# Pooled half first: a mix that starts before the heads are scaled, in a two-layer decoder trunk

## What is computed

```python
h = rmsnorm(x, norm1)
proj = h @ w_in                                  # q, k, v, o: 4 x 512; u_pool: 512; 8 gates
hm = mlstm(q, k, v, gates, state)                # 4 heads of width 128
hm = hm * lax.rsqrt(jnp.mean(hm * hm, axis=-1, keepdims=True) + EPS)
hm = hm.reshape(B, T, MLSTM_WIDTH) * mlstm_norm * o
zp = pool_mixer(u_pool, ...)                     # windows 2/4/8/16, w_pool, pool_scale
mix = jnp.concatenate([hm, zp], axis=-1) @ w_out # 1024 -> 1024
x = x + mix
x = x + peer_ffn(rmsnorm(x, norm2), ...)         # 8 heads x 16 of 16384 experts for each token
x = x + sigmoid(x @ w_gate) * (p @ w_ple)
```

## Time and profile before

| | |
|---|---|
| median of 3 runs | 1942.24 us (1940.42 to 1944.46) |
| the profiled execution | 1939.56 us, its span 1937.8 us |
| busy share of the span | PE 53%, DVE 57%, ACT 9%, POOL 60% |
| TensorE clock granted, mean | 0.762 of full speed |
| chain that ended last | DMA 32%, POOL 24%, PE 17%, DVE 15%, issue 11% |
| moved | 687.24 MB, 553.72 MB of it by the gathers |

### The profile page before, as it was taken

The page is one execution under the profiler, slowest core; times in us unless marked ns, Lnnn a source line. Parts: engine busy times, 40 slices in busy tenths (PEclk is TensorE's granted clock), DMA queues, the critical chain, the costliest instruction groups (busy, mean ns, idle before and its releaser), DMA issues.

```text
span 1937.8 us, 18049 instructions
## 1 busy us (share of the span) xinstructions
PE 1034.4 (53%) x6274; PEld 477.3 (25%) x6274; DVE 1095.3 (57%) x2851; ACT 173.9 (9%) x297; POOL 1156.0 (60%) x1062
## 2 busy tenths in 40 slices
PE   7867230574754654717655766465854640035556
PEld 3433120332311232304111333332311120021113
DVE  1266898867920467888800486968950179960001
ACT  2222010000100011100000022101100010000001
POOL 0033556254677766676677767456576787777770
PEclk9888665687878876758778978777876675568888
DMA  7577767697999999999999999899799999999993
GB/s 294 190 297 283 260 223 283 181 380 294 385 409 409 409 413 412 372 377 353 410 409 409 405 407 408 275 359 399 256 401 410 409 404 409 409 409 409 409 409 144
DMA packets 173192, 687.24 MB, mean 355 GB/s; under 512 B 19856, under 2 KB 21520, under 8 KB 158366
## 3 DMA queue, kind: packets, MB, share of 16 engines
q0 software_dynamic: 152064, 553.72, 73.1%
q1 hardware_dynamic: 21038, 132.37, 18.0%
HBM read 679.88 MB, written 6.59 MB: 354 GB/s over the span
## 4 chain that ended last, share of the span: by engine, by line
DMA 32%; POOL 24%; PE 17%; DVE 15%; issue 11%; ACT 1%; SPq 0%; DVEq 0%; ACTq 0%; POOLq 0%
POOL rows L1182 24%; DMA rows<-in_v,index_tb 10%; DMA rows<-in_u,index_A 7%; PE bank L728 7%; DMA rows<-in_v,index_ta 7%; PE acc L1010 6%; DMA rows<-in_u,index_B 4%; DVE rows L1747 4%; DMA wring<-in_w 1%; DVE scratch L1570 1%; DMA rows<-in_v,index_S 1%; DVE scratch L1644 1%; PE bank L725 1%; DVE scratch L1694 1%; DVE scratch L1693 1%
## 5 line engine op out<-in xcount | busy, mean ns | idle before, releaser
L1182 POOL DMA_INDIRECT rows<-in_u,index_A x256 | 325.3, 1271 | 365.6 <-DVE index_A L1722 178.4
L1010 PE MATMUL acc<-rows,wz 128*32 128x512 f32 x2048 | 341.4, 798 | 289.2 <-DMA rows<-in_v,index_tb 142.8
L728 PE MATMUL bank<-wring,turned 128*128 128x512 f32 x832 | 410.3, 645 | 69.9 <-DVE decayed L1454 33.0
L1182 POOL DMA_INDIRECT rows<-in_u,index_B x256 | 299.8, 1171 | 108.8 <-issue 71.0
L1747 DVE SCALAR_TENSOR_TENSOR rows<-rows,xn_a 128x1024 f32<-128x1024 f32 x256 | 304.7, 1224 | 79.9 <-DMA rows<-in_u,index_A 76.6
L1182 POOL DMA_INDIRECT rows<-in_v,index_ta x256 | 252.6, 987 | 145.0 <-PE acc L1010 78.2
L1747 DVE SCALAR_TENSOR_TENSOR rows<-rows,xn_b 128x1024 f32<-128x1024 f32 x256 | 306.9, 1226 | 56.7 <-DMA rows<-in_u,index_B 51.1
L1182 POOL DMA_INDIRECT rows<-in_v,index_tb x256 | 242.3, 946 | 107.7 <-issue 61.9
L728 PEld LDWEIGHTS bank<-wring,turned 128*128 128x128 f32 x832 | 165.6, 208 | 272.5 <-issue 245.9
L1010 PEld LDWEIGHTS acc<-rows,wz 128*32 128x32 f32 x2048 | 74.0, 127 | 532.9 <-issue 510.7
L1780 DVE TENSOR_TENSOR x_b<-x_b,acc 128x1024 f32<-128x1024 f32 x2 | 2.4, 1222 | 260.6 <-PE acc L1010 260.6
(11 more groups left out here) (293 smaller groups left out, 997.5 us busy)
## 6 DMA issues: line engine op xcount, KB each, us to landing
wring<-in_w SPq DMA_DIRECT2D x108, 1024.0 KB, 8.1
scratch<-in_c_s SPq DMA_DIRECT2D x2, 2064.0 KB, 11.1
out_c_s<-scratch SPq DMA_DIRECT2D x2, 2064.0 KB, 9.9
rows<-in_u,index_A POOLq DMA_INDIRECT x256, 11.4
rows<-in_v,index_ta POOLq DMA_INDIRECT x256, 7.7
rows<-in_u,index_B POOLq DMA_INDIRECT x256, 9.2
rows<-in_v,index_tb POOLq DMA_INDIRECT x256, 7.9
keys<-in_keys SPq DMA_DIRECT2D x2, 1024.0 KB, 9.8
```

The source lines that it names most:

```text
L728: ins = pe.matmul(ps[:, :], turned["A"][:, 4 * h + c, :], w[:, c, :], start=first, stop=end, skip_group_check=True)
L1010: ins = pe.matmul(acc[i * QUAD:(i + 1) * QUAD, c, :], wz[:, i, g * QUAD:(g + 1) * QUAD], row, start=first, stop=end, skip_group_check=True)
L1182: pool.indirect_dma_start(out=rows[:, n % RING, :], out_offset=None, in_=a[table], in_offset=bass.IndirectOffsetOnAxis(ap=which[:, at:at + ...
```

## The change

In the mix, half h = 0 becomes the pooled inputs and half h = 1 the heads: `half_index` swaps the two halves of the weights for the mix, and `dense` reads the other half of `turned`. The mix's first block now waits for the pooling alone; the wait for the heads moves to `(j, h) == (0, 1)`. In the list of pass 0, the h = 0 halves of both blocks stand ahead of `scale_heads` and `heads`. In the other passes `scale_heads` of the large tile goes behind `weigh_keys`, pooling goes ahead of the sample tile's `scale_heads` and `heads`, and the halves (0, 0) of the mix go ahead of these too. The planner's tables are unchanged, `dense` takes one source, and its waits are otherwise as before.

```diff
@@ stage_front
     add("norm_heads", big)
-    add("scale_heads", big)
     if p:
         add("weigh_keys", big)
     else:
         add("pool_r", big)
         add("pool", big)
+        for j in range(2):
+            add("mix", p, j, 0, big)
+    add("scale_heads", big)
     add("heads", big)
...
         add("norm_heads", t)
-        add("scale_heads", t)
-        add("heads", t)
     for t in tiles if p else []:
         add("pool_r", t)
     for t in tiles if p else []:
         add("pool", t)
-    for j in range(2):
-        for h in range(2):
-            for t in tiles:
-                add("mix", p, j, h, t)
+    for t in tiles if p else []:
+        add("mix", p, 0, 0, t)
+    for t in small:
+        add("scale_heads", t)
+        add("heads", t)
+    for j, h in ((0, 1), (1, 0), (1, 1)) if p else ((0, 1), (1, 1)):
+        for t in tiles:
+            add("mix", p, j, h, t)
@@ half_index
-    return {"project": IN0, "mix": OUT0, "query": PQ0, "gate": GATE0}[e[0]] + 2 * e[2] + e[3]
+    h = 1 - e[3] if e[0] == "mix" else e[3]
+    return {"project": IN0, "mix": OUT0, "query": PQ0, "gate": GATE0}[e[0]] + 2 * e[2] + h
@@ dense
-                        for s in source:
-                            for i in range(1 if kind == "S" or not parts else parts):
-                                emptied(pe, *((s, t, i) if parts else (s, t)))
+                        for i in range(1 if kind == "S" else parts):
+                            emptied(pe, *((source, t, i) if parts > 1 else (source, t)))
...
+                chunk = 4 * (1 - h if name == "mix" else h)
...
-                        ins = pe.matmul(ps[:, :], turned["A"][:, 4 * h + c, :], w[:, c, :], start=first, stop=end,
+                        ins = pe.matmul(ps[:, :], turned["A"][:, chunk + c, :], w[:, c, :], start=first, stop=end,
@@ mix
-                dense("mix", p, j, h, t, ("heads", "pool_z"), 0)
+                if (j, h) == (0, 1):
+                    emptied(pe, "heads", t)
+                dense("mix", p, j, h, t, "pool_z", 1)
```

More of the change, by code:

```diff
@@ L724, in dense @@
                         for g in range(4):
-                            ins = pe.matmul(ps[lane_group(g), 0:P], turned["S"][:, 4 * h + c, :], w[:, c, g * P:(g + 1) * P],
+                            ins = pe.matmul(ps[lane_group(g), 0:P], turned["S"][:, chunk + c, :], w[:, c, g * P:(g + 1) * P],
                                             start=first, stop=end, skip_group_check=True)
                     else:
-                        ins = pe.matmul(ps[:, :], turned["A"][:, 4 * h + c, :], w[:, c, :], start=first, stop=end,
+                        ins = pe.matmul(ps[:, :], turned["A"][:, chunk + c, :], w[:, c, :], start=first, stop=end,
                                         skip_group_check=True)
@@ L767, in project @@
             def project(p, j, h, t):
-                dense("project", p, j, h, t, ("turn",), 2)
+                dense("project", p, j, h, t, "turn", 2)
             def cumulate(t):
@@ L909, in query @@
             def query(p, j, h, t):
-                dense("query", p, j, h, t, ("turn2",), 2)
+                dense("query", p, j, h, t, "turn2", 2)
             def turn_pq(t, j):
@@ L1018, in gate @@
             def gate(p, j, h, t):
-                dense("gate", p, j, h, t, ("turn3",), 2)
+                dense("gate", p, j, h, t, "turn3", 2)
             def embed(p):
```

## The result

The changed kernel takes 1949.86 us (median of 20 runs, 1944.21 to 1957.09) and the kernel before, in the runs beside it, 1940.53 us (20 runs, 1936.61 to 1948.46). The forecast was +9.0 us and 1951.2 us. The profiled execution of the changed kernel took 1945.72 us, its span is 1943.9 us, at a mean granted clock of 0.767.

The account below looks back on a forecast made before the run. It took the DMA engines, full at about 410 GB/s, as the bound, so only longer dry times of the gather queue cost. 0.6 + 2.3 + 6.5 - 0.7 + 0.3 = +9.0 on 1942.24 gave 1951.2 us, range 1944.5 to 1957.5.

Parts of the forecast that it names:

- Pass 2's v group, +6.5: Tile 1's first v group waits 16.7 us longer for wz, 10.2 us is refunded: +6.5 us, ends 0 and +16.7.
- The refund: Pass 2: four weight halves travel while the gathers stand still, instead of inside the v stream, giving back 10.2 us.
- Pass 2's earlier mix, -0.7: Pass 2: mix starts some 1.35 us earlier, second addition 0.6 us late, so 0.7 us kept; ends 0 and 3.
- Pass 0, +0.6: Pass 0's mix starts 0.86 us earlier, but head transposes in its middle add 1.50 us; ends +0.3 and +1.5.
- the upper end: Pass 0: transposes stay at the slow 1.06 us and the earlier start buys one more slow matmul pass, 0.43 us: +1.5.
- Pass 1, +2.3: Pass 1: dots ahead of the last choose delay the states' load, store and mix weights by 2.3 us; ends 0 and +3.
- Pass 3, +0.3: Pass 3: mix starts no sooner, one PE transpose costs +0.3 us, engines stay full; ends -12 and +5.1.
- a sign of a wrong forecast: Pass 3's last u row moving by over 3 us more than pass 2's end does.
- the third rival: Pass 3 loses its four rows too, +5.1 us: +14.1 in all, 1956.3 us; chance 0.14.
- the rule on the shared port: VectorE and GpSimd share an exclusive port pair, causing Pool's long issues; by it pass 3 would give 1956 us.
- the fourth rival: Passes 2 and 3: row products fill waits, turn2 comes earlier in pass 3, 12.3 us there: -5.6, 1936.6 us; chance 0.07.
- The rate of 410 GB/s: Gathers and weight halves move at about 410 GB/s when engines have work: 1.28 us a gather, 2.56 a half.

Follow-up runs that it names:

- e3: Changed kernel with the new list in pass 2 alone, the old list in passes 0, 1 and 3; 1949.40 us, ratio 1.0039 to before.
- e9: Changed kernel, with gelu and copy into wz of tile 1 and the small tile, and tile 1's first v group, taken at once; 1944.74 us, ratio 1.0027.
- e10: Kernel before, with tile 1's copy into wz and first three v groups moved behind four ranks, pairs, two best and a query block; 1955.23 us, ratio 1.0081.
- e7: Kernel before, plus a planner rule taking each tile's gelu and copy into wz the moment they can be; 1927.44 us, ratio 0.9925.
- e1: Changed kernel with the new list in pass 0 alone, the old list in passes 1, 2 and 3; 1939.26 us, ratio 0.9993 to before.
- e2: Changed kernel with the new list in pass 1 alone, the old list in passes 0, 2 and 3; 1936.45 us, ratio 0.9979 to before.
- e5: Changed kernel with the old list in all four passes, so only the exchange of the mix's halves is kept; 1938.43 us, ratio 1.0000 to before.
- e8: Kernel before, plus a planner rule taking each tile's gelu, copy into wz and first v group at once; 1910.81 us, ratio 0.9864.
- e4: Changed kernel with the new list in pass 3 alone, the old list in passes 0, 1 and 2; 1939.13 us, ratio 0.9983 to before.
- e12: Kernel before, plus a planner rule taking each tile's gelu, copy into wz and first three v groups at once; 1920.15 us, ratio 0.9900.

## Why the prediction was right, and where its steps were not

- **The whole.** +9.0 forecast, +7.8 (5.2 to 10.3) measured; 1951.2 us against 1949.86. Pass 2 carries it, as forecast; that the sum came so close is in part luck, as the last point says.
- **Pass 2's v group, +6.5: right in place and mechanism; the size agrees, with a second wait in it.** First v group 920.32 (forecast near 923), waiting for wz; Pool standing over 20 us in all, in two pieces. Late by 17.1 us counted from the last u row, where I had 16.7; given back 9.4, where I had 10.2; left 7.7 of dry time, and +7.6 us measured for the pass alone (e3). The step lacked one thing: the dots of the sample tile come later too. They are inside the 17.1, but in e9, with wz in time and the first v group only 2.4 us late, 4.7 us stay (9.7 against 5.0 dry), where late by 2.4 with no half carried would make 2.4 by my working. e10 shows that both terms depend on their neighbours: the same copy made late by hand cost +15.7, for it was 23.2 us late and brought two halves forward, not four.
- **The refund and the queues.** It agrees with the Trainium skill (DMA: Bandwidth & Descriptors, Issuing engines are not separate DMA queues) in both cases: 9.4 us for four halves, 3.9 for two, at 2.56 each.
- **Pass 2's earlier mix, -0.7: not shown.** The mix starts at 785.84 against 789.68, but the whole pass ran ahead there. Counted from DVE's copy into `last_mb` just before the heads (773.78, now 772.28), it starts 2.3 us earlier and turn2 (801.56, was 806.92) 3.9; in e3 it is 1.4 and 0.3, where I had 1.35 and 0.7. From the pass's first gather to its last u row the four traces with the new list in pass 2 take 243.2 to 245.8 us and the ten without 242.1 to 247.8, so no gain can be told.
- **Pass 0, +0.6: inside its ends.** The step was transposes and wait, 1.50 less 0.86, and those were right at 1.45 and 0.85. The rest is the clock, which I had only in the upper end. The mix starts at 1.2 GHz in both kernels, and 2.4 GHz comes at 73.98 us before and at 73.19 in the changed kernel, 16.6 and 16.3 us behind the transposes: the clock rises hardly sooner for the earlier start, and the sixteen products take 0.54 us more. From those transposes to turn2 the four traces with the new list in which the clock rises between 72.9 and 74.3 us have 30.2 to 30.5 us (mean 30.4), the three with the old list and the old halves in which it rises between 73.0 and 74.5 have 29.0 to 29.5 (mean 29.3): +1.1. Over all five of each kind it is 30.2 and 28.4, but in e7 and e10 the clock was back at 68.3, with the same order as before there. e1's -1.4 (-4.7 to +1.9) can't tell any of this.
- **What the exchange does by itself in pass 0.** With the exchange of the halves and the old list (e2 to e5) the same stretch is 26.6 to 27.2 us (mean 26.9): the mix follows the head transposes at once, since it needs only the pooled half. Against that, by the means of all traces, the new list costs 3.3 us there, and the exchange alone gains 1.5; much of both is that the clock was back sooner in these four: with it back at 68.3 us in all three, e3 has 26.6 us and e7 and e10 27.1. In the whole time e5 is 0.0 (-3.1 to +3.3), too coarse to show it.
- **Pass 1, +2.3: wrong.** The group of dots does stand ahead of the choose. But Pool had been standing, for 22.36 us before and 21.39 after, and these dots free two of its slots sooner. Before, its wait ended with DVE's row products behind the choose, and in the changed kernel with the choose itself:

```profile
350.06 1.18 POOL L1182 DMA_INDIRECT rows<-in_u,index_A  x1 [22.36 <-DVE rows L1747]
```

```profile
348.86 1.80 POOL L1189 DMA_INDIRECT rows<-in_u,index_A  x1 [21.39 <-DVE index_A L1729]
```

  The first weight half arrived hardly later. Changed kernel, SP and PE, to be read against the earlier trace rows:

```profile
348.61 0.33 SPq L1121 DMA_DIRECT2D scratch<-in_c_s  x1
...
393.64 5.58 PE L733 MATMUL bank<-wring,turned 128*128 128x512 f32 x8 [11.85 <-DMA wring<-in_w]
```

  From the load of the states to the mix it is 45.03 us, and it was 46.46. The load stands at 348.61 and not near 351 only because the pass ran ahead: counted from DVE's copy into `last_mb` (326.42, now 324.93) it comes 2.05 us later, as forecast, but the mix only 0.6. The dry time from the 97th u row to the last is 16.9 to 18.0 in the five traces with the new list in pass 1, and 17.9 to 21.1 in the nine without: a gain of about 2 us, not a loss of 2.3; e2, the pass alone, is at -4.1 (-7.0 to -1.2). The lower end that I had named was 0, and it was not low enough: I had priced the chain that is pushed back, and not the ring slots that pushing it back releases.
- **Pass 3, +0.3: the wrong way, by some 2 us.** Its last u row came 3.6 us later than the shift at the end of pass 2 (10.84 against 7.23), which I had named as a sign of a wrong forecast. The 13th v row is 7.05 us later than before, so the 3.6 are back at once: the sign was badly chosen. The stretch from the 97th u row to the 33rd v row has 18.2 us dry after and 21.9 before; without the rule of e7 and e8 the four traces with the new list in pass 3 have 18.2 to 19.2, the six without 19.4 to 21.9. e4, the pass alone, is at -3.3 (-6.4 to 0.0). Both point to a gain of some 2 us; what brings it was not tried. So the third rival (+5.1, four rows lost) falls, and with it the forecast that the rule on the shared port of the Trainium skill (SBUF — State Buffer, Who interferes with whom) would have given (Pool's issues from 1300 to 1345 us took 0.93 to 1.99 us again, median 1.21 where it was 1.68); the fourth rival asked for -12 here and falls too.
- **The sum.** Read from the traces, the terms are +1.1, about -2, +7.7 and about -2, some +5 in all, where the forecast's were +0.6, +2.3, +5.8 and +0.3. The misses in passes 1 and 3 go the same way, about 4 and 2 us, and those in passes 0 and 2 make up for less than half of them. The measured +7.8 (5.2 to 10.3) lies above that, by less than single traces vary. The rate of 410 GB/s behind every price held; that 409 or 410 stands in half of the slices was misread, it is 14 of 40.

## What to carry to other kernels

When a kernel is bound by a gather ring, ask of every reordering what stands on the consumer's engine between the last use of one stream and the first use of the next; here that toll came back as lost time, less about the time of the weight halves that travelled meanwhile (17.1 us less 9.4, 23.2 less 3.9). Count dry time (length x (1 - GB/s / peak)) between the same two gathers of both kernels: it adds up to the difference of the spans when both move the same bytes, and says in which stretch the difference lies, where shares of busy time do not. It needs several traces: one stretch of unchanged work varied by 7.7 us. And a place where a change makes things worse is worth a search for the same place elsewhere: passes 1 and 3 had carried a larger toll all along, and taking it out (e8) brought 26.4 us.

## What the runs showed of the hardware

An earlier start on PE is worth less while the granted clock is low. Tables of stretches, pass 0, 68 to 76 us (column before the last two: granted clock; the full 2.4 GHz is 1.00, 1.2 GHz is 0.50), of the kernel before, the changed one and e5:

```profile
68.00:76.00 8.00, 7.10 (x14) 3.15 (x13) 1.38 (x2) 0.00 (x0) 0.00 (x0) 0.63 0.00 0
```

```profile
68.00:76.00 8.00, 7.70 (x13) 3.37 (x14) 1.07 (x3) 0.00 (x0) 0.00 (x0) 0.68 0.08 13
```

```profile
68.00:76.00 8.00, 7.95 (x19) 3.61 (x18) 1.34 (x2) 0.00 (x0) 0.00 (x0) 0.84 0.20 60
```

PE had been waiting for ACT (4.79 us ahead of the pooling's product), and the clock had fallen. In e5, with the exchange alone, the mix runs straight on from the head transposes and starts at 68.75; its 16 products take 14.86 us, and from the transposes at 57.31 to turn2 it is 27.20. There the clock is back at 2.4 GHz at 70.55 us. In the changed kernel the products start 0.45 us earlier, behind a pause of 0.90 us, and the clock is back at 73.19. In the four traces with e5's list and halves in pass 0 it is back between 68.3 and 70.6 us, in the five with the changed kernel's between 71.9 and 74.3. That the pause is the reason is not shown: before, e7, e8, e10 and e12 have it too, and there the clock was back at 68.3 in two and at 73.0 to 74.5 in three. Among kernels with the same order in pass 0 that stretch still varies from 27.1 to 29.5 us. The Trainium skill (TensorE: Matmul & The Clock Gate, Part 1: The HAM clock gate) says that the number of slow matmuls after an idle time varies from run to run; the traces agree, with these 2.4 us: of the mix's 32 records none started at 1.2 GHz in e7 and e10, and five or six in before, e8 and e12.
